# Forget gates' logits from four column tiles of 32 columns in place of a weight chunk of 128

## The reference

```python
mod = jax.nn.silu(c) @ w_ada[l] + b_ada[l]
shift, scale, gate = jnp.split(mod, 3, axis=-1)
h = rms_norm(x, g_pre[l]) * (1.0 + scale[:, None, :]) + shift[:, None, :]
proj = h @ w_in[l]
qa, ka, va, fa, za, qb, kb, vb, zb = jnp.split(proj, split_points, axis=-1)
...
cum = jnp.cumsum(jax.nn.log_sigmoid(fa + b_fgate[l]), axis=1)
...
s = s + cb[..., None] - cum[:, :, None, :]   # added to the scores of forgetting attention
```

## Time and profile before

| what | value |
|---|---|
| median of 3 runs | 1152.31 us (1152.17 to 1152.65) |
| the profiled execution: its own time | 1153.57 us |
| its span, first to last instruction | 1151.8 us |
| TensorE busy | 1124.1 us, 98% |
| VectorE busy | 819.5 us, 71% |
| ScalarE busy | 585.8 us, 51% |
| GpSimd busy | 66.2 us, 6% |
| mean granted clock of TensorE | 0.996 |

### The profile page before, as it was taken

One profiled execution on the slowest core, in us unless ns is written; L12 is line 12 of the kernel. 1 busy time (PEld: TensorE's weight loads), 2 busy tenths in 40 slices (PEclk: granted clock), 3 DMA queues, 4 the chain that ended last, 5 costly groups with the idle time before them and its releaser, 6 DMA issues.

```text
span 1151.8 us, 15721 instructions
## 1 busy us (share of the span) xinstructions
PE 1124.1 (98%) x5796; PEld 919.5 (80%) x5796; DVE 819.5 (71%) x1424; ACT 585.8 (51%) x1084; POOL 66.2 (6%) x73
## 2 busy tenths in 40 slices
PE   5899999999999999999999999999999999999998
PEld 5898777766898877877778778888888888788887
DVE  5788655668566347999999985898777787853342
ACT  6663555456565455766766663325553223651230
POOL 2019500101000000000000000000000000000000
PEclk9899999999999999999999999999999999999999
DMA  9967422321355322212222242323223333223221
GB/s 343 353 218 256 128 72 74 92 65 38 129 169 197 109 75 73 74 38 92 74 92 74 72 145 96 110 77 106 74 74 98 123 98 104 92 73 110 93 72 73
DMA packets 35276, 130.20 MB, mean 113 GB/s; under 512 B 4272, under 2 KB 4656, under 8 KB 34688
## 3 DMA queue, kind: packets, MB, share of 16 engines
q1 hardware_dynamic: 31536, 112.74, 29.3%
q0 software_dynamic: 3376, 16.23, 4.2%
q10 hardware_dynamic: 288, 0.24, 0.1%
HBM read 121.59 MB, written 6.29 MB: 111 GB/s over the span
## 4 chain that ended last, share of the span: by engine, by line
PE 89%; DVE 5%; ACT 3%; DMA 2%; issue 2%; SPq 0%; POOL 0%; DVEq 0%; ACTq 0%
PE bank L475 27%; PE bank L477 26%; PE bank L476 26%; PE bank L726 2%; PE bank L577 2%; DMA raw<-in_chunks 2%; PE bank L847 2%; PE bank L754 1%; DVE wl L1813 1%; PE bank L680 1%; ACT qf L1211 1%; DVE stat L1969 0%; DVE cumt L2502 0%; ACT wh L1130 0%; PE bank L716 0%
## 5 line engine op out<-in xcount | busy, mean ns | idle before, releaser
L475 PE MATMUL bank<-hl,wh 128*128 128x512 f32 x888 | 357.9, 403 | 0.0
L477 PE MATMUL bank<-hh,wh 128*128 128x512 f32 x888 | 347.0, 391 | 0.0
L476 PE MATMUL bank<-hh,wl 128*128 128x512 f32 x888 | 346.2, 390 | 0.0
L1813 DVE TENSOR_TENSOR wl<-raw,wh 128x1024 fp32r<-128x1024 f32 x185 | 225.1, 1238 | 103.8 <-ACT wh L1130 103.0
L1130 ACT ACTIVATE wh<-raw 128x1024 fp32r<-128x1024 f32 x185 | 192.0, 1058 | 205.8 <-PE bank L477 186.3
L475 PEld LDWEIGHTS bank<-hl,wh 128*128 128x128 f32 x888 | 167.1, 188 | 36.6 <-issue 3.1
L477 PEld LDWEIGHTS bank<-hh,wh 128*128 128x128 f32 x888 | 166.7, 188 | 36.2
L476 PEld LDWEIGHTS bank<-hh,wl 128*128 128x128 f32 x888 | 167.2, 188 | 31.3 <-issue 0.7
L2225 DVE SCALAR_TENSOR_TENSOR ca<-u,vt,ca 128x512 f32<-128x512 f32 x232 | 157.9, 746 | 0.0
L476 PE MATMUL bank<-oh,wl 128*128 128x512 f32 (+1 forms) x256 | 94.0, 367 | 0.0
L477 PE MATMUL bank<-oh,wh 128*128 128x512 f32 (+1 forms) x256 | 93.9, 367 | 0.0
(11 more groups left out here) (337 smaller groups left out, 1649.1 us busy)
## 6 DMA issues: line engine op xcount, KB each, us to landing
raw<-in_chunks SPq DMA_DIRECT2D x193, 512.0 KB, 3.6
ada_a<-in_chunks SPq DMA_DIRECT2D x8, 512.0 KB, 11.6
ada_b<-in_chunks SPq DMA_DIRECT2D x8, 512.0 KB, 9.5
x<-in_x POOLq DMA_DIRECT2D x4, 512.0 KB, 10.5
mem_scratch<-kvm POOLq DMA_DIRECT2D x1, 2048.0 KB, 9.5
x<-in_x POOLq DMA_DIRECT2D x1, 2048.0 KB, 8.5
x_scratch<-x POOLq DMA_DIRECT2D x1, 2048.0 KB, 7.7
kvm<-mem_scratch POOLq DMA_DIRECT2D x1, 2048.0 KB, 9.3
```

The costliest lines, as they stand in the source:

```text
L475: pe.matmul(o, a[0], b[1], start=start, stop=False, **kw)
L476: pe.matmul(o, a[1], b[0], start=False, stop=False, **kw)
L477: return pe.matmul(o, a[0], b[0], start=False, stop=stop, **kw)
L1813: dve.tensor_tensor(wl[:, w], raw[:, RAW_SLOT[nxt]], wh[:, w].bitcast(F32), ALU.subtract)\
```

## The change

The chunk `fa` is gone. The 8 x 1024 gate weights are packed behind the small vectors and loaded once, in float32, into `fgate` (128 x 8 x 32, 128 KB), together with `fours` (128 x 128, 64 KB), a pattern that is 1 where row and column agree modulo 32. Both loads are issued by GpSimd near the start. After `qa 0` TensorE multiplies four column tiles of 32 columns: column tile `part` takes chunks 2 `part` and 2 `part` + 1 of the features, unsplit float32 (`xT`), so that each holds a partial sum over a quarter of the features. ScalarE copies the bank into `cumt`, and after the first step of `va` a matmul with `fours` adds the four partial sums in bank 6. The logarithms follow from there on, behind `va` chunks in ScalarE's and VectorE's orders. GpSimd's load of `sel`, and what follows in its queue, waits for the column tiles to be done, because `sel` and the angles lie where `xT` is.

As `CHUNKS` has one entry less and `ADA_BEHIND` is as it was, the order from 16 on becomes `qa 0`, `va 0` (pieces 16, 17), `va 1`, `va 2` (18, 19), `va 3`, `ka 0` (20, 21), `za 0`, `qa 1` (22, 23), `ka 1`, `zb 0` and so on: the pieces follow the same position, and so the next chunk.

```diff
-CHUNKS += [("fa", 0), ("qa", 0)] + [("va", j) for j in range(4)] + [("ka", 0)]
+CHUNKS += [("qa", 0)] + [("va", j) for j in range(4)] + [("ka", 0)]
...
+            def gate_logits():
+                pe.wait_ge(s.fours_in, 32)
+                b = next_bank()
+                banks.open(pe, b, "fa")
+                for i in range(2):
+                    for part in range(4):
+                        c, rows = 2 * part + i, slice(32 * part, 32 * part + 32)
+                        ins = pe.matmul(ps[b][rows, :], fgate[:, c, :], xT[:, c], start=i == 0, stop=i == 1,
+                                        skip_group_check=True)
+                banks.close(ins, "fa")
-            chunk(("fa", 0), H, split=s.h_lo)
-            chunk(("qa", 0), H)
-            wide("va", 0, H, [(tt, (2, 3, 4, 7)[tt]) for tt in range(T)])
+            chunk(("qa", 0), H, split=s.h_lo)
+            gate_logits()
+            tiles = [(tt, (2, 3, 4, 7)[tt]) for tt in range(T)]
+            for s_ in range(4):
+                if s_ == 1:
+                    banks.wait_empty(pe, "fa")
+                    banks.open(pe, 6, "logits")
+                    banks.close(pe.matmul(ps[6][:], fours[:], cumt[:, 1, :], start=True, stop=True), "logits")
+                used(wide_step("va", 0, s_, H, tiles), "va", 0, s_, tiles)
             chunk(("ka", 0), H)
             pe.wait_ge(s.ada_used, 24)
...
+            pool.dma_start(fours[:], t["consts"][:, K_FOURS:K_FOURS + P]).then_inc(s.fours_in, 16)
+            pool.dma_start(fgate[:].rearrange("p c n -> p (c n)"), t["vectors"][:, VT_COLS:]).then_inc(s.fours_in, 16)
...
             pool.wait_ge(s.h_lo, 8)
+            banks.wait_full(pool, "fa")
             pool.dma_start(sel[:].rearrange("p a n -> p (a n)"), ...
...
             banks.wait_empty(act, ("qa", 0))
             split_q(0)
+            f, e, l, cum = (cumt[:, n, :] for n in range(4))
+            banks.wait_full(act, "fa")
+            banks.empty(act.activation(e, ps[banks.where["fa"][0]][:], ACT.Copy), "fa")
+            ahead(("qa", 0))
             act.wait_ge(s.kvm_out, 16)
+            ahead(("va", 0))
+            act.wait_ge(s.cum_dve, 1)
+            act.activation(e, f, ACT.Abs).then_inc(s.cum_act, 1)
...
+            act.activation(e, e, ACT.Ln, bias=ones[:, 0:1]).then_inc(s.cum_act, 1)
+            ahead(("va", 1))
             act.wait_ge(s.cum_dve, 2)
             act.activation(negcum[:], cum, ACT.Copy, scale=-1.0).then_inc(s.cum_hi, 1)
-            for s_ in range(3):
-                ahead(("va", s_))
+            ahead(("va", 2))
...
             split_q(0, 1)
+            ahead(("va", 0))
+            banks.wait_full(dve, "logits")
+            banks.empty(dve.tensor_scalar(f, bank("logits")[:], fbias, None, ALU.add), "logits")
+            banks.wait_empty(dve, "logits")
+            dve.memset(l, 1.0).then_inc(s.cum_dve, 1)
+            dve.wait_ge(s.cum_act, 3)
+            then(dve.scalar_tensor_tensor(e, f, 0.0, e, ALU.min, ALU.subtract))
+            dve.tensor_tensor_scan(cum, l, e, 0.0, ALU.mult, ALU.add).then_inc(s.cum_dve, 1)
+            ahead(("va", 1))
             dve.wait_ge(s.cum_hi, 1)
```

More of the change, by code:

```diff
@@ L52 @@
 K_DIST = 385 + 4 * P
-K_COLS = K_DIST + S
+K_FOURS = K_DIST + S
+K_COLS = K_FOURS + P
 VEC_ROWS = [("c", 8), ("b_ada", 16), ("g_pre", 8), ("norm_g", 8), ("mem_g", 8), ("dw_b", 8), ("ln_g", 8),
@@ L146 @@
 SIGNALS = {
-    "ones_in": "ones loaded", "sq_hi": "differential outputs' squares: hi", "sq_lo": "lo",
+    "ones_in": "ones loaded", "fours_in": "forget gates' weights and the pattern that adds four partial sums loaded",
+    "sq_hi": "differential outputs' squares: hi", "sq_lo": "lo",
     "const_in": "identity and frequencies loaded", "rows_in": "packed vectors loaded",
@@ L231, in constants @@
     back = i[:, None] + (S - P) - np.arange(S)[None, :]
+    k[:, K_FOURS:K_FOURS + P] = (i[:, None] % 32) == (i[None, :] % 32)
     k[:, K_DIST:K_DIST + S] = np.where(back >= 0, -0.5 * back, MASKED)
@@ L241, in packed_vectors @@
            "dkn": "diff_kn_g_2", "subln": "diff_subln_g_2", "xqn": "x_qn_g_2", "xkn": "x_kn_g_2"}
-    vt = np.zeros((P, VT_COLS), np.float32)
+    vt = np.zeros((P, VT_COLS + 32 * C), np.float32)
+    gates = np.asarray(inputs["w_in"])[0][:, 1536:1544].reshape(C, P, 8)
+    vt[:, VT_COLS:].reshape(P, C, 32)[:, :, 0:8] = gates.transpose(1, 0, 2)
     for name, (at, count) in VEC.items():
@@ L250, in packed_vectors @@
     taps = np.asarray(inputs["conv_dw_2"])[0].reshape(TAPS, C, P)
-    vt[:, NVEC:] = taps.transpose(2, 0, 1).reshape(P, TAPS * C)
+    vt[:, NVEC:VT_COLS] = taps.transpose(2, 0, 1).reshape(P, TAPS * C)
     return vt
@@ L275, in packed_chunks @@
             a = w_out_2[:, cols]
[L276 to L279, removed]
         elif kind in ("qb", "zb"):
@@ L379, in build @@
         ident_b = sb("ident_b", [P, P], BF16)
-        dist, blocks, xk = shared([("dist", [P, S], F32), ("blocks", [P, P], F32)], [("xk", [P, 2, 2, MEM], F32R)])
+        dist, blocks, fours, fgate, xk = shared([("dist", [P, S], F32), ("blocks", [P, P], F32), ("fours", [P, P], F32),
+                                     ("fgate", [P, C, 32], F32)], [("xk", [P, 2, 2, MEM], F32R)])
         vt = sb("vt", [P, VT_COLS])
@@ L1215, in _ @@
             act.dma_start(cst[:], t["consts"][:, 0:K_ONES]).then_inc(s.const_in, 16)
-            act.dma_start(vt[:], t["vectors"]).then_inc(s.rows_in, 16)
+            act.dma_start(vt[:], t["vectors"][:, 0:VT_COLS]).then_inc(s.rows_in, 16)
             act.wait_ge(s.eps_done, 1)
@@ L1282, in _ @@
                 ahead(("mv", 2 * g + 1))
[L1284 to L1292, removed]
             def raw_q(key, i, free, next_=True):
@@ L1300, in raw_q @@
                     ahead(key)
-            raw_q(("qa", 0), 0, 0)
+            raw_q(("qa", 0), 0, 0, False)
             def split_q(c):
@@ L1323, in _ @@
             split_q(0)
+            f, e, l, cum = (cumt[:, n, :] for n in range(4))
+            banks.wait_full(act, "fa")
+            banks.empty(act.activation(e, ps[banks.where["fa"][0]][:], ACT.Copy), "fa")
+            ahead(("qa", 0))
             act.wait_ge(s.kvm_out, 16)
+            ahead(("va", 0))
+            act.wait_ge(s.cum_dve, 1)
+            act.activation(e, f, ACT.Abs).then_inc(s.cum_act, 1)
+            act.wait_ge(s.cum_act, 1)
+            act.activation(e, e, ACT.Exp, scale=-1.0).then_inc(s.cum_act, 1)
+            act.wait_ge(s.cum_act, 2)
+            act.wait_ge(s.ones_in, 16)
+            act.activation(e, e, ACT.Ln, bias=ones[:, 0:1]).then_inc(s.cum_act, 1)
+            ahead(("va", 1))
             act.wait_ge(s.cum_dve, 2)
             act.activation(negcum[:], cum, ACT.Copy, scale=-1.0).then_inc(s.cum_hi, 1)
-            for s_ in range(3):
-                ahead(("va", s_))
+            ahead(("va", 2))
             for tt in range(T):
@@ L1894, in _ @@
             f, e, l, cum = (cumt[:, n, :] for n in range(4))
[L1895 to L1903, removed]
             banks.wait_full(dve, ("qa", 0))
```

## The result

The changed kernel takes 1161.17 us (median of 4 runs, 1160.88 to 1162.6), the kernel before 1152.24 in runs beside it (4 runs, 1151.31 to 1152.65): ratio 1.0082, 95% interval 1.0066 to 1.0098. It is 8.9 us slower, where the prediction had +3.65 and a range that ended at 1159.5. The profiled execution after has 1160.92 us and a span of 1159.1, 7.3 more than the span before.

The account below looks back on a forecast made before the run. TensorE was taken to bound the kernel, holding 89% of the chain that ended last. Stall 1.85, loads 0.6 and clock 1.2 gave +3.65 us: 1157.2 profiled, 1155.9 for the median, range 1149.9 to 1159.5.

Parts of the forecast that it names:

- The chain: From the column tiles through GpSimd's queue, store, ScalarE and VectorE to piece 23: 32.5 us, gate's matmuls 1.85 us later.
- All upper bounds of the prediction together: Tiles to piece 23 with every link at its upper bound: +2.6 us, 1158.5, inside the likeliest case's range.
- Tiles and pattern: On TensorE, 2.0 us for eight tile matmuls and 0.86 for the pattern replace `fa`'s 5.46: -2.6 us.
- Rival (c): Column tiles do not run four at a time: 1157.6 with two together, 1161.0 one by one; chance 0.13.
- I take 9.5, the store itself: The 2 MB store of the memory's keys and values, from issue at 90.6 to landing: 9.5 us.
- The bound of 0.8 above 9.5: 384 KB of loads just ahead in the store's queue may add 0.8 us to its landing.
- I take 5.2: VectorE's one rest and two pieces, priced between 4.4 and 6.1 us, used twice in the way to piece 23.
- The clock: TensorE's idling before the gate lowers its granted clock: 2.0 us lost, 0.8 absorbed, so +1.2 us.
- rival (a): The stall ahead of the gate comes without loss of clock: +2.45 us, 1154.8; chance 0.21.
- The loads at the start: `fours` and `fgate`, 192 KB issued at about 18 us, delay TensorE's stream: +0.6 us.
- The median: The profiled execution before is 1.26 us above the median, so 1157.2 became 1155.9.
- Rival (b): No stall ahead of the gate, the 2.6 us gain stands less 0 to 0.6: 1149.7 to 1150.3; chance 0.22.

Follow-up runs that it names:

- the 36 matmuls: The changed kernel with 36 matmuls without use run on TensorE ahead of its wait for piece 23: 1159.37 us, ratio 1.0052.
- all links short: The changed kernel with pieces ordered by name, ScalarE's store wait only ahead of `va`'s copies, logarithms ahead of `ka`'s split: 1152.0 us, ratio 1.000.
- the kernel before with the moved slot: The kernel before, with the planner's skipped slot taken at the second `ka` chunk of the fill, not the first `wo` chunk: 1153.87 us, ratio 1.0008.

## Why the prediction was wrong

The mechanism came as forecast; wrong is the size of one term: "The chain is 32.5 us from 89.0, and TensorE is there at 117.05. It idles 4.4 us". Measured: 37.1 us from 88.03, TensorE there at 116.41, 8.79 us idle. All upper bounds of the prediction together gave 2.6 us more; 4.6 more came. Against the profiled executions, +3.65 was forecast and +7.35 came (1153.57 to 1160.92).

- **Tiles and pattern, right.** 2.05 us with both sides (2.0 predicted), and the pattern's matmul has the predicted two records and pushes what follows by 0.87 us. The saving is 2.4 us by the traces (2.6 predicted). Rival (c) is out; that its price for tiles one by one, 1161.0, is nearly the measured time is chance. The Trainium skill ("TensorE: Matmul & The Clock Gate", Part 3, Packing small matmuls) has 2.38 times for three tiles, so 0.79 of ideal; by this trace four tiles reach 8 x 0.86 / 1.85 = 3.7 of 4, so 0.93, and the measurement decides.
- **"I take 9.5, the store itself", wrong by 2.2.** The store was priced from an issue at 86.87, ahead of the chunks that SyncE's queue moves at 88 to 92 us, and with no load of its own queue just ahead of it. Behind both, it landed after 11.7 us, and after 11.9 to 13.1 in the seven other kernels that issue it there. Issued at 85.7 to 86.9, as in the kernel before, it took 8.3 to 9.5 in five traces. The bound of 0.8 above 9.5 left out SyncE's chunks, and it priced the 384 KB of the small loads at the store's 0.49 MB in one us; they moved at 0.20, which the earlier trace rows has for q0, too.
- **"I take 5.2", wrong twice by 0.75.** Between 4.4 and 6.1 the middle was taken. The change moves both triples into GpSimd's angles; they ran at 5.95 each, near the dear end, whose row was known. Without GpSimd's arithmetic they take 3.7.
- **GpSimd's wake, missing.** 0.76 us pass from the tiles' end to its first issue. The other links agree with their prices within 0.5 us: together 37.1 - 32.5 = 4.6 is these 2.2 + 1.5 + 0.8 and 0.1 over.
- **The clock, right.** 1.2 was predicted: 2.0 lost, 0.8 absorbed. By the start of the first probabilities (128.68, 135.52 after, now without idle time) the lag grew from 5.55 to 6.84 us, so by 1.29. That the stall was twice as long as forecast does not make this luck: behind stalls of 2.32 to 4.34 us the loss was 1.7 to 2.4. That the loss is the clock is shown by the 36 matmuls, so rival (a) is out. The Trainium skill ("TensorE: Matmul & The Clock Gate", Part 1, The HAM clock gate) has it that idling brings TensorE to half clock; the granted 0.50 behind the stall agrees.
- **The loads at the start, wrong.** +0.6 was predicted. The first matmul behind the second idle time starts at 33.13 instead of 33.31; it lies between 32.95 and 33.63 in the ten kernels with the loads, and between 33.31 and 33.37 in three traces without them. The 192 KB cost nothing that can be seen. The tiles start at 86.11, 0.9 sooner than predicted, and from 85.40 to 87.13 in the ten kernels. This goes with the clock, which differs from execution to execution: in the stretch from 33 to 39 us it was 0.66 here and 0.50 before. With all links short, so with the loads, it was 0.50 and the tiles started at 87.13; in the kernel before with the moved slot, so without them, it was 0.72 and `qa` started at 85.89.
- **The median.** 1.26 us were taken off because the profiled execution before stood above its median; the one after stands 0.25 below its own. This made the miss of 3.7 one of 5.3.
- **Not thought of.** The planner's skipped slot and the turn of probabilities at 269 us (277 in the changed kernel). TensorE waits there 1.1 us in the changed kernel and not at all before, but the skipped slot is not shown to be the cause in that kernel. Part of the wait is made up elsewhere, as the lag grows from 6.84 at the first probabilities to 7.3 at the end.

Rival (b), no stall, hung on the store and on VectorE's triples. In the runs the waits at the gate and at the scores go only with the order restored, the wait for the store out of the chain and the logarithms taken earlier; then the saving stands at 121 us, and with `wo` split as before 2.0 us of it at the end.

Open: how long the rotation's swap takes. From issue to VectorE's next step it was 3.3 us in both traces before, 4.2 and 4.4 in the two kernels that split `wo` as before, and 5.2 to 5.6 in five kernels with the early split; the two of these shown have a chunk's load (512 KB) beside it in the trace. But the changed kernel has that load beside its swap, too, and VectorE went on after 4.4 without waiting, as in three other kernels with the early split. So the load is not all of it, and nothing here shows why 3.3 became 4.2 without one. Open, too, is how the store's 2.2 us divide between SyncE's chunks and the loads of its own queue.

## What to carry to other kernels

A saving on the bounding engine is worth what the next wait leaves of it: follow the producer's order on the other engines, and price each link at the load of its new place, not at that of its old one. Removing an item from a list that others index by position moves them all; look for slot parities and hand-written positions, and restore them by name. And where a chain has several links of similar weight, shortening one moves the wait; it went only when several were taken out together.

## What was not expected of the hardware

VectorE's steps on 128 x 1024 took 1.2 to 1.34 us alone and 1.6 to 2.2 beside GpSimd's tensor work. GpSimd's queue moved one packet in a microsecond in which SyncE's queue moved 93, and a 2 MB store landed after 8.3 to 9.5 or after 11.7 to 13.1 us by what was in flight or queued ahead of it at its issue. An idle time of 8.8 us on TensorE cost another 2.0 us through the granted clock, and one of 2.3 us cost 1.7.
